# A blocked triangular inverse for two scan directions: one direction's right factor moved to the other partition half, its products to the off-diagonal array quarters

## The chip, the cores and the metric

The kernel runs on one core of a Trainium2 chip, in one launch. A core has TensorE (PE), VectorE (DVE), ScalarE (ACT), GpSimd (POOL) and SyncE (SP, which issues the DMAs here). The metric is device time in microseconds (us) of the whole kernel.

## What is computed

Two layers of an encoder over two sequences of 256 tokens, width 1024, in float32. Layer 0 mixes tokens by a linear recurrence in both directions, layer 1 by attention; a gated MLP follows each. Only the recurrence matters here. For each of 16 heads of 64 channels, and for each direction:

```python
def step(S, inp):
    r_t, w_t, k_t, v_t, a_t, b_t = inp
    sa = jnp.einsum('bhij,bhj->bhi', S, a_t)
    S = S * w_t[:, :, None, :] + sa[..., None] * b_t[:, :, None, :] + v_t[..., None] * k_t[:, :, None, :]
    return S, jnp.einsum('bhij,bhj->bhi', S, r_t)
...
y = (_wkv_scan(r4, dec4[0], kd4[0], v4, -kk, kk * a4[0], reverse=False)
     + _wkv_scan(r4, dec4[1], kd4[1], v4, -kk, kk * a4[1], reverse=True))
```

## The kernel before

Activations lie transposed, channels on the 128 partitions, the 512 tokens of both sequences along the free dimension. A pair of heads fills the partitions: the first head has partitions 0 to 63, the second 64 to 127 (`halves`). The recurrence is worked in chunks of 64 tokens (`NCH` = 8). Within a chunk it is a unit triangular system of 64 x 64, for every chunk, head and direction `n`, and its inverse is built in five levels (`LEVELS`) that double the size of the inverted blocks. Three 64 x 64 matrices per chunk and direction take part: `nt` is the system, `mt` the inverse so far transposed, `mc` the inverse so far, and `xc` holds the masked product between them. One level is: `xc` = mask(`nt`^T `mc`), the system product (`level_system`, L753 to L762); new `mc` = `mt`^T `xc`, the factor product (`level_factors`, L772); new `mt` = `xc`^T `mt`, the transposed factor (L778, not at the last level). Ahead of level 0 `first_factors` (L744) transposes `mt` into the first `mc`.

Each product is, for one direction, 16 calls of 64 x 64 x 64 in float32: 8 chunks times two heads. The profile has two matmul instructions for each call. A call reads both operands from one head's 64 partitions and writes the same 64 partitions of PSUM, so it uses one of the two diagonal 64 x 64 quarters of the array. Direction 0 goes to PSUM bank 4 (`mt`: bank 2), direction 1 to bank 5 (bank 3).

The other engines take the results out. DVE multiplies `xc` out of PSUM with a mask (L1778) and copies direction 1's `mt` (L1806). ACT copies both `mc` (L1309 for the first, L1322) and direction 0's `mt` (L1328); at the last level the result is `mf` (L1325). POOL makes the first `mt` from the system (`ident`, L1999 and L2002).

The pairs of heads run through a pipeline of stages, `stage(i)`, written out by hand for each engine: stage i scans pair i (`scans`), solves the triangular system of pair i+1 (`solves`), prepares pair i+2 (`prepares`) and normalises the output of pair i-1 (`norms_`). Every engine works in the order written. Between the products of a level PE does pieces of the scan (`solved`, `next_state`, `from_state`, `outputs`) and of the preparation (`key_scales` L675, `lora_rates` and `lora_decays` L659, `bonus_sum` L695); DVE and ACT do likewise (sigmoids L1254, exponentials from L1275, scans L1682 and L1687, the bonus L1698 and L1701, the prepared factors L1712 to L1717). At the end of a stage `grams` (L796, L800) and `transposed` (L814) make the operands of the next scan.

Six stages also carry two halves of an adaLN modulation: a matrix product L556 (`modulation_half`), an ACT copy of its row, a selection on PE (L710, `select_half`), and an ACT copy of the columns. Its weights come through one buffer, which SP fills again when a half's matmuls are done. All of these, the key scales, the LoRA products and the bonus sum share PSUM bank 7, and `key_scales` waits until the modulation columns of the stage before have been copied (`ada_taken`).

## Time and profile before

| | us |
|---|---|
| median of 3 runs | 2025.67 |
| lowest and highest | 2021.66, 2025.8 |
| the profiled execution | 2024.68 |
| its span, first to last instruction | 2022.9 |
| recurrence stages, first system product to the last stage | 252.7 to about 845 |
| one full stage (system product to system product) | 72.5 to 74.9 |

In the rows further down, L-numbers are lines of the kernel before; "PEld" is a weight load, "PE" a matmul. A matmul row of the timeline covers instructions of one line and form that follow each other: its start, its time to the end of the last one, their count (x32 is 16 calls). The number in brackets is how long the engine had been idle and what released it. Instructions of TensorE overlap, so that a row's time includes the tail of its last instruction, and the distance between the starts of two rows is what the first of them takes of the engine's time. The granted clock is a share of 2.4 GHz; it is 1.00 or 0.50.

### The profile page before, as it was taken

To read this page: it belongs to the slowest core of one execution; us is meant where nothing else is said; L and a number is where in the kernel's file an instruction comes from. 1 tells how busy PE (TensorE), PEld (TensorE's weight loads), DVE (VectorE), ACT (ScalarE), POOL (GpSimd) and SP (SyncE) were. 2 spreads that over 40 slices of the span, in tenths; PEclk is the share of its full clock that TensorE was granted. 3 is DMA by queue.
4 is the path that set the end of the run, shared out by engine and by line. 5 is a ranking of instruction groups with operands and counts; after the bars stand their busy time and mean duration, and the time that the engine had idled before them with its cause. 6 is when DMAs were issued, how large, how long until landed. Compare 5 with 4: busy or idle time off the path is not lost.

```text
span 2022.9 us, 45036 instructions
## 1 busy us (share of the span) xinstructions
PE 1782.7 (88%) x19956; PEld 1419.1 (70%) x19956; DVE 888.0 (44%) x1127; ACT 720.3 (36%) x1096; POOL 609.7 (30%) x314
## 2 busy tenths in 40 slices
PE   5999589899999899787999999978686789999995
PEld 2777278788888789564777788855565568888884
DVE  3755544454454454426333442035674454444203
ACT  3322233333333332235433332224343354444221
POOL 1332222222222220033333344443111434434433
PEclk8999789999999999898999999989798889999998
DMA  7330000110110100143556233211111213333221
GB/s 293 94 124 21 26 7 7 45 40 18 45 50 8 44 26 5 47 164 146 213 202 246 76 101 112 93 36 47 36 32 42 73 52 93 93 93 105 100 86 42
DMA packets 43881, 161.08 MB, mean 80 GB/s; under 512 B 3664, under 2 KB 18256, under 8 KB 40912
## 3 DMA queue, kind: packets, MB, share of 16 engines
q1 hardware_dynamic: 43728, 158.75, 23.0%
q8 instruction: 132, 2.16, 0.5%
q14 instruction: 21, 0.17, 0.0%
HBM read 156.64 MB, written 2.10 MB: 78 GB/s over the span
## 4 chain that ended last, share of the span: by engine, by line
PE 79%; DVE 11%; ACT 4%; POOL 3%; issue 2%; DMA 1%; ACTq 0%; DVEq 0%; SPq 0%; POOLq 0%
PE ps L529 14%; PE ps L530 14%; PE ps L531 14%; PE ps L772 4%; PE ps L778 3%; PE ps L760 2%; PE ps L630 2%; PE ps L631 2%; PE ps L632 2%; PE ps L556 2%; PE ps L814 2%; DVE x_res L1534 2%; PE ps L796 1%; DVE area L1464 1%; DVE area L1874 1%
## 5 line engine op out<-in xcount | busy, mean ns | idle before, releaser
L1952 POOL TENSOR_TENSOR split_w<-raw_w,split_w 128x1024 fp32r<-128x1024 f32 (+1 forms) x148 | 380.6, 2571 | 743.2 <-ACT split_w L1118 743.2
L530 PE MATMUL ps<-h_lo_pad,split_w 128*128 128x512 f32 x800 | 321.3, 402 | 0.0
L529 PE MATMUL ps<-h_hi,split_w 128*128 128x512 f32 x704 | 283.4, 403 | 17.7 <-DVE h_lo_pad L1473 17.7
L1118 ACT ACTIVATE split_w<-raw_w 128x1024 fp32r<-128x1024 f32 (+1 forms) x148 | 167.2, 1130 | 355.8 <-PE ps L531 355.6
L531 PE MATMUL ps<-h_hi,split_w 128*128 128x512 f32 x704 | 279.5, 397 | 0.0
L529 PE MATMUL ps<-ff_hi,split_w 128*128 128x512 f32 x448 | 178.8, 399 | 8.9 <-DVE h_lo_pad L1473 8.9
L529 PEld LDWEIGHTS ps<-h_hi,split_w 128*128 128x128 f32 x704 | 133.8, 190 | 68.8 <-issue 29.1
L531 PE MATMUL ps<-ff_hi,split_w 128*128 128x512 f32 x448 | 175.8, 393 | 0.0
L530 PEld LDWEIGHTS ps<-h_lo_pad,split_w 128*128 128x128 f32 x800 | 152.1, 190 | 33.7 <-issue 0.5
L1548 DVE SCALAR_TENSOR_TENSOR ffs<-ffs,fcur 128x512 f32<-128x512 f32 x44 | 82.5, 1876 | 176.5 <-ACT ffs L1151 176.5
L531 PEld LDWEIGHTS ps<-h_hi,split_w 128*128 128x128 f32 x704 | 133.0, 189 | 31.9
L1513 DVE TENSOR_TENSOR sx<-sx,ffs 128x512 f32<-128x512 f32 x32 | 22.2, 693 | 289.1 <-ACT ffs L1086 289.1
L530 PE MATMUL ps<-ff_lo,split_w 128*128 128x512 f32 x352 | 136.9, 389 | 0.0
L529 PEld LDWEIGHTS ps<-ff_hi,split_w 128*128 128x128 f32 x448 | 84.9, 190 | 30.7 <-issue 9.2
L772 PEld LDWEIGHTS ps<-area 64*64 64x64 f32 x2560 | 88.3, 144 | 17.1 <-issue 16.6
L772 PE MATMUL ps<-area 64*64 64x64 f32 x2560 | 95.8, 229 | 4.0 <-DVE area L1778 3.8
L531 PEld LDWEIGHTS ps<-ff_hi,split_w 128*128 128x128 f32 x448 | 84.8, 189 | 18.4
L1991 POOL TENSOR_TENSOR split_p<-o_res,split_p 128x1024 fp32r<-128x1024 f32 x24 | 57.9, 2413 | 129.3 <-ACT split_p L1229 129.3
L630 PE MATMUL ps<-x_split,split_p 128*128 128x512 f32 x192 | 78.4, 408 | 18.6 <-DVE x_split L1608 10.1
L1322 ACT ACTIVATE area<-ps 128x512 f32<-128x512 f32 x64 | 38.2, 597 | 147.8 <-PE ps L772 147.8
L760 PEld LDWEIGHTS ps<-area 64*64 64x64 f32 x2560 | 79.2, 136 | 10.6 <-issue 10.6
L1556 DVE TENSOR_TENSOR ffs<-ffs,ps 128x512 f32<-128x512 f32 x44 | 30.3, 688 | 123.6 <-ACT ffs L1155 123.6
(255 smaller groups left out, 3248.7 us busy)
## 6 DMA issues: line engine op xcount, KB each, us to landing
raw_w<-in_ffn_up SPq DMA_DIRECT2D x88, 512.0 KB, 3.7
raw_w<-in_ffn_down SPq DMA_DIRECT2D x32, 704.0 KB, 4.0
late_a<-in_ada_w SPq DMA_DIRECT2D x7, 2048.0 KB, 8.1
late_b<-in_ada_w SPq DMA_DIRECT2D x7, 2048.0 KB, 8.0
o_res<-in_proj_w SPq DMA_DIRECT2D x24, 512.0 KB, 3.7
area<-in_ada_w SPq DMA_DIRECT2D x12, 1024.0 KB, 6.1
area<-in_ada_w SPq DMA_DIRECT2D x4, 2048.0 KB, 21.2
x_res<-in_xT SPq DMA_DIRECT2D x2, 2048.0 KB, 11.4
```

The lines of the kernel that those rows point to most:

```text
L529: mm(bank, wh[:, o:o + P], hi[:, t], start=(t == 0), stop=False)
L530: mm(bank, wh[:, o:o + P], lo[:, t], start=False, stop=False)
L531: last = mm(bank, wl[:, o:o + P], hi[:, t], start=False, stop=(t == total - 1))
L556: last = mm(bank[g:g + CG, :], csil[:, k, :], blk[:, k, :], start=(k < NCG), stop=(k >= KT - NCG))
L630: mm(ps[:, m, :], wh[:, o:o + P], xh, start=(k == 0), stop=False)
L760: last = mm(ps[lo:hi, 4 + n, c * C:(c + 1) * C], nt[lo:hi, n, c, :], mc[lo:hi, n, c, :], start=True, stop=True)
L772: last = mm(ps[lo:hi, 4 + n, c * C:(c + 1) * C], mt[lo:hi, n, c, :], xc[lo:hi, n, c, :], start=True, stop=True)
L778: last = mm(ps[lo:hi, 2 + n, c * C:(c + 1) * C], xc[lo:hi, n, c, :], mt[lo:hi, n, c, :], start=True, stop=True)
L1118: A(split_w[:, r % 2, 0, 0:cols], raw_w[:, r, 0:cols], ACT.Copy).then_inc(w_hi, 1)
L1548: own(V.scalar_tensor_tensor(seqs(conv[s]), u_pad[s][:, :, 0:SEQ], fcur[:, s, 0:1], seqs(conv[s]), ALU.mult, ALU.add))
L1952: G.tensor_tensor(split_w[:, r % 2, 1, 0:cols], raw_w[:, r, 0:cols], split_w[:, r % 2, 0, 0:cols].bitcast(F32), ALU.subtract).then_inc(w_l ...
L1991: G.tensor_tensor(split_p[:, n % 2, 1], raw_p[:, n % NRAW, :], split_p[:, n % 2, 0].bitcast(F32), ALU.subtract).then_inc(proj_lo, 1)
```

## The change

For direction 1 the masked product `xc` and the factor `mt` lie on the other partition half: what belongs to the first head is on partitions 64 to 127, and the reverse. `nt` and `mc` stay. So direction 1's system product reads one half and writes the other, and its factor product goes back; both use the off-diagonal quarters. The calls of the two directions alternate, and the two last of them signal. The first `mt` of direction 1 is made by POOL in `xc`, brought to the other half by 16 products with the identity, and copied by DVE into `mt`. Bank 5 has what direction 1 writes across, bank 4 what direction 0 writes.

Other work is moved. On PE the first modulation half leaves level 4 and stands behind `outputs`, the second stands behind `transposed`, and the second selection stands in level 0 of the next stage, ahead of `key_scales`; ACT's copies move with them. The bonus of pair 0 on PE and DVE moves from ahead of the stages into the first stage.

```diff
+        across = ((0, C, C, P), (C, P, 0, C))
...
             def first_factors(q):
...
+                pe.wait_ge(ident_in, 2 * q + 2)
+                for c in range(NCH):
+                    o = slice(c * C, (c + 1) * C)
+                    for lo, hi, a, b in across:
+                        swapped = mm(ps[a:b, 5, o], ident[lo:hi, lo:hi], xc[lo:hi, 1, c, :], start=True, stop=True)
+                        last = mm(ps[lo:hi, 3, o], xc[lo:hi, 1, c, :], ident[lo:hi, lo:hi], start=True, stop=True)
+                    if c == NCH - 1:
+                        swapped.then_inc(side_mm, 1)
+                last.then_inc(mmm[1], 1)
 
             def level_system(q, l):
 
                 for n in range(NDIR):
                     pe.wait_ge(mev[n], LEVELS * q + l + 1)
-                    for c in range(NCH):
-                        for lo, hi in halves:
-                            last = mm(ps[lo:hi, 4 + n, c * C:(c + 1) * C], nt[lo:hi, n, c, :], mc[lo:hi, n, c, :],
-                                      start=True, stop=True)
-                    last.then_inc(xmm[n], 1)
+                if l == 0:
+                    pe.wait_ge(side_in, q + 1)
+                for c in range(NCH):
+                    o = slice(c * C, (c + 1) * C)
+                    for lo, hi, a, b in across:
+                        one = mm(ps[lo:hi, 4, o], nt[lo:hi, 0, c, :], mc[lo:hi, 0, c, :], start=True, stop=True)
+                        two = mm(ps[a:b, 5, o], nt[lo:hi, 1, c, :], mc[lo:hi, 1, c, :], start=True, stop=True)
+                one.then_inc(xmm[0], 1)
+                two.then_inc(xmm[1], 1)
...
             def level_factors(q, l):
...
                     pe.wait_ge(xev[n], LEVELS * q + l + 1)
-                    for c in range(NCH):
-                        for lo, hi in halves:
-                            last = mm(ps[lo:hi, 4 + n, c * C:(c + 1) * C], mt[lo:hi, n, c, :], xc[lo:hi, n, c, :],
-                                      start=True, stop=True)
-                    last.then_inc(mmm[n] if l < LEVELS - 1 else fmm[n], 1)
-                    if l < LEVELS - 1:
+                for c in range(NCH):
+                    o = slice(c * C, (c + 1) * C)
+                    for lo, hi, a, b in across:
+                        one = mm(ps[lo:hi, 4, o], mt[lo:hi, 0, c, :], xc[lo:hi, 0, c, :], start=True, stop=True)
+                        two = mm(ps[a:b, 5, o], mt[lo:hi, 1, c, :], xc[lo:hi, 1, c, :], start=True, stop=True)
...
+                if q == 0:
+                    bonus_sum(0)
...
+                        if 0 <= b < ADA_PAIRS:
+                            select_half(2 * b + 1)
                         if prepares:
                             key_scales(r)
...
-                        if ada_:
-                            modulation_half(2 * p)
...
-                    elif ada_:
-                        select_half(2 * p)
                 if scans:
                     outputs(p)
                 if ada_:
-                    modulation_half(2 * p + 1)
+                    modulation_half(2 * p)
                 if solves:
                     grams(q)
                 if ada_:
-                    select_half(2 * p + 1)
+                    select_half(2 * p)
                 if solves:
                     transposed(q)
+                if ada_:
+                    modulation_half(2 * p + 1)
...
+                if solves:
+                    dve.wait_ge(side_mm, q + 1)
+                    V.tensor_copy(mt[:, 1], chunks(ps[:, 5, :])).then_inc(side_in, 1)
                 for l in range(LEVELS):
...
-                    G.tensor_tensor(mt[:, n], nt[:, n], m1, ALU.mult).then_inc(ident_in, 1)
+                    G.tensor_tensor(xc[:, 1] if n else mt[:, 0], nt[:, n], m1, ALU.mult).then_inc(ident_in, 1)
```

In the following rows a count is of calls; the sizes are those of the output. PE at level 0 of the stage that starts at 611 us, before: L760 is the system product, L860 a piece of the scan, L724 the variance of the pair before, L675 the key scales, L772 and L778 the factor product and the transposed factor of direction 0, then of direction 1.

```order
L760 MATMUL ps<-area 64x64 x32
L860 MATMUL ps<-area 64x64 x8
L724 MATMUL ps<-area,ct 128x512
L675 MATMUL ps<-area 128x256 x2
L772 MATMUL ps<-area 64x64 x16
L778 MATMUL ps<-area 64x64 x16
L772 MATMUL ps<-area 64x64 x16
L778 MATMUL ps<-area 64x64 x16
```

The same place after the change; L772 and L773 (now the system product of direction 0 and of 1) and L786 and L787 (the factor product) alternate to 16 calls each, of which the last two and the first two stand here. L876, L726 and L677 are L860, L724 and L675.

```order
L772 MATMUL ps<-area 64x64
L773 MATMUL ps<-area 64x64
L876 MATMUL ps<-area 64x64 x8
L726 MATMUL ps<-area,ct 128x512
L712 MATMUL ps<-ct,area 128x2 x2
L677 MATMUL ps<-area 128x256 x2
L786 MATMUL ps<-area 64x64
L787 MATMUL ps<-area 64x64
```

The products of the two directions stand call by call in turn, and a selection (L712) stands between the variance and the key scales.

PE at level 4 and the end of the same stage, before: L841 is the scan, L556 and L710 the modulation, L772 the last factor product, L872 to L884 the outputs, L796 and L800 the grams, L814 the transposes.

```order
L841 MATMUL ps<-area 64x64 x8
L556 MATMUL ps<-area,csil 32x256 x8
L772 MATMUL ps<-area 64x64 x32
L710 MATMUL ps<-ct,area 128x2 x2
L872 MATMUL ps<-x_res,sx 64x64 x24
L878 MATMUL ps<-area 64x64 x32
L884 MATMUL ps<-area 64x64 x32
L556 MATMUL ps<-area,csil 32x256 x8
L796 MATMUL ps<-area 64x128 x32
L800 MATMUL ps<-area 64x64 x32
L710 MATMUL ps<-ct,area 128x2 x2
L814 MATMUL ps<-ct,area 64x64 x80
```

After the change, from the outputs (L888) on:

```order
L888 MATMUL ps<-x_res,sx 64x64 x24
L894 MATMUL ps<-area 64x64 x32
L900 MATMUL ps<-area 64x64 x32
L558 MATMUL ps<-area,csil 32x256 x8
L812 MATMUL ps<-area 64x128 x32
L816 MATMUL ps<-area 64x64 x32
L712 MATMUL ps<-ct,area 128x2 x2
L830 MATMUL ps<-ct,area 64x64 x80
L558 MATMUL ps<-area,csil 32x256 x8
L742 MATMUL ps<-x_res 64x64 x32
```

Ahead of the outputs there is now no modulation and no selection between the scan and the last factor product; one modulation half stands between the outputs and the grams, and the other between the transposes and the next system product.

## Rows read from the trace of the kernel before

**Rows 1.** The page, part 4: the chain that ended last, by engine.
```profile
PE 79%; DVE 11%; ACT 4%; POOL 3%; issue 2%; DMA 1%; ACTq 0%; DVEq 0%; SPq 0%; POOLq 0%
```
**Rows 2.** Busy us by stage: stretch, length, each engine (instructions), clock, DMA.
```profile
252.70:315.80 63.10, 53.27 (x1328) 48.88 (x1328) 27.94 (x44) 20.64 (x33) 15.74 (x12) 0.86 0.03 6
...
463.90:536.40 72.50, 66.96 (x1852) 59.22 (x1852) 36.39 (x57) 26.32 (x45) 16.30 (x12) 1.00 0.12 36
...
611.00:685.10 74.10, 68.52 (x1852) 60.72 (x1852) 36.40 (x57) 26.39 (x45) 16.30 (x12) 0.98 0.11 35
...
685.10:758.50 73.40, 67.22 (x1852) 59.38 (x1852) 36.39 (x57) 26.32 (x45) 16.30 (x12) 1.00 0.06 19
```
**Rows 3.** Timeline, level 0 of the stage at 611 us: start, us, engine, line, operation, count [idle].
```profile
618.21 1.15 PE L750 MATMUL ps<-ct,area 64*64 64x64 f32 x32 [1.13 <-POOL area L2002]
...
619.19 2.03 PE L760 MATMUL ps<-area 64*64 64x64 f32 x64
...
619.41 0.60 ACT L1309 ACTIVATE area<-ps 128x512 f32<-128x512 f32 x1 [1.68 <-PE ps L750]
...
621.06 0.63 PE L860 MATMUL ps<-area 64*64 64x64 f32 x16
```
**Rows 4.** Timeline, products on row halves and column groups.
```profile
613.48 1.12 PE L719 MATMUL ps<-o_res,ct 128*128 128x512 f32 x2
...
628.40 1.13 PE L659 MATMUL ps<-area 64*128 64x512 f32 x4
...
662.14 1.07 PE L556 MATMUL ps<-area,csil 128*32 128x256 f32 x16 [2.71 <-DVE area L1701]
```
**Rows 5.** Timeline, level 4 of that stage: evictions, factor product, select.
```profile
659.87 1.28 DVE L1778 TENSOR_TENSOR area<-ps,ct 128x512 f32<-128x512 f32 x2
...
663.14 3.46 PE L772 MATMUL ps<-area 64*64 64x64 f32 x64
...
666.53 0.75 PE L710 MATMUL ps<-ct,area 128*128 128x2 f32 x4
```
**Rows 6.** Timeline, level 1: PE behind the sigmoids.
```profile
632.24 0.68 PE L841 MATMUL ps<-area 64*64 64x64 f32 x16 [0.70 <-ACT h_pad L1254]
```
**Rows 7.** Timeline, level 2: evictions and factor product.
```profile
641.32 1.28 DVE L1778 TENSOR_TENSOR area<-ps,ct 128x512 f32<-128x512 f32 x2
...
642.15 1.15 PE L772 MATMUL ps<-area 64*64 64x64 f32 x32
```
**Rows 8.** Timeline, level 3: system product, second eviction, bonus sum.
```profile
647.77 2.08 PE L760 MATMUL ps<-area 64*64 64x64 f32 x64
...
649.89 0.69 DVE L1778 TENSOR_TENSOR area<-ps,ct 128x512 f32<-128x512 f32 x1 [0.24 <-PE ps L760]
...
651.63 1.12 PE L695 MATMUL ps<-h_pad,ct 128*128 128x512 f32 x2 [0.25 <-DVE h_pad L1698]
```
**Rows 9.** Timeline, start of the stage.
```profile
611.00 2.08 PE L740 MATMUL ps<-area 64*64 64x64 f32 x64 [0.70 <-ACT area L1355]
```
**Rows 10.** DMA issues: target, queue, count, KB each, median us to landing.
```profile
area<-in_ada_w SPq DMA_DIRECT2D x12, 1024.0 KB, 6.1
```
**Rows 11.** Timeline, stage at 758.5 us: first system product, last factor product.
```profile
766.69 2.03 PE L760 MATMUL ps<-area 64*64 64x64 f32 x64
...
800.41 2.03 PE L772 MATMUL ps<-area 64*64 64x64 f32 x64
```
**Rows 12.** Timeline, stage at 252.7 us: last factor product.
```profile
298.98 3.68 PE L772 MATMUL ps<-area 64*64 64x64 f32 x64 [3.15 <-DVE area L1778]
```
**Rows 13.** Timeline, ahead of the stage at 252.7 us and into it.
```profile
247.85 0.69 DVE L1701 SCALAR_TENSOR_TENSOR area<-ps,area 128x512 f32<-128x512 f32 x1 [2.17 <-PE ps L695]
...
248.84 1.79 POOL L2021 TENSOR_TENSOR x_res<-h_pad 128x512 f32<-128x512 f32 x1
...
252.71 3.68 PE L740 MATMUL ps<-x_res 64*64 64x64 f32 x64 [4.90 <-DVE x_res L1717]
...
258.16 1.97 PE L750 MATMUL ps<-ct,area 64*64 64x64 f32 x32 [1.77 <-POOL area L2002]
```

More of the change, by code:

```diff
@@ L333, in encoder_trunk @@
         tr, tr_in, ident_in = sem("tr"), sem("tr_in"), sem("ident_in")
+        side_mm, side_in = sem("side_mm"), sem("side_in")
         xmm, xev, mmm, mev = (pair_of(n) for n in ("xmm", "xev", "mmm", "mev"))
@@ L744, in first_factors @@
             def first_factors(q):
-                for n in range(NDIR):
-                    pe.wait_ge(ident_in, 2 * q + n + 1)
-                    for c in range(NCH):
-                        for lo, hi in halves:
-                            last = mm(ps[lo:hi, 2 + n, c * C:(c + 1) * C], mt[lo:hi, n, c, :], ident[lo:hi, lo:hi],
-                                      start=True, stop=True)
-                    last.then_inc(mmm[n], 1)
+                pe.wait_ge(ident_in, 2 * q + 1)
+                for c in range(NCH):
+                    for lo, hi in halves:
+                        last = mm(ps[lo:hi, 2, c * C:(c + 1) * C], mt[lo:hi, 0, c, :], ident[lo:hi, lo:hi], start=True, stop=True)
+                last.then_inc(mmm[0], 1)
+                pe.wait_ge(ident_in, 2 * q + 2)
[7 more added lines that the diff above has]
+                last.then_inc(mmm[1], 1)
             def level_system(q, l):
@@ L769, in level_factors @@
                     pe.wait_ge(xev[n], LEVELS * q + l + 1)
-                    for c in range(NCH):
-                        for lo, hi in halves:
-                            last = mm(ps[lo:hi, 4 + n, c * C:(c + 1) * C], mt[lo:hi, n, c, :], xc[lo:hi, n, c, :],
-                                      start=True, stop=True)
-                    last.then_inc(mmm[n] if l < LEVELS - 1 else fmm[n], 1)
-                    if l < LEVELS - 1:
+                for c in range(NCH):
+                    o = slice(c * C, (c + 1) * C)
+                    for lo, hi, a, b in across:
+                        one = mm(ps[lo:hi, 4, o], mt[lo:hi, 0, c, :], xc[lo:hi, 0, c, :], start=True, stop=True)
+                        two = mm(ps[a:b, 5, o], mt[lo:hi, 1, c, :], xc[lo:hi, 1, c, :], start=True, stop=True)
+                one.then_inc(mmm[0] if l < LEVELS - 1 else fmm[0], 1)
+                two.then_inc(mmm[1] if l < LEVELS - 1 else fmm[1], 1)
+                if l < LEVELS - 1:
+                    for n in range(NDIR):
                         for c in range(NCH):
@@ L972, in _ @@
             lora_rates(0, (7, 1))
-            bonus_sum(0)
             for i in range(-1, KT + 1):
@@ L1300, in stage @@
                 ada_ = scans and prepares
+                if 0 <= b < ADA_PAIRS:
+                    modulation_row(2 * b + 1)
                 if scans:
@@ L1310, in stage @@
                 for l in range(LEVELS):
+                    if l == 0 and 0 <= b < ADA_PAIRS:
+                        modulation_columns(2 * b + 1)
                     if l == 0 and norms_:
@@ L1315, in stage @@
                         right_sides(p, 2)
-                    if l == 4 and ada_:
-                        modulation_row(2 * p)
                     if solves:
@@ L1342, in stage @@
                     elif l == 4:
-                        if ada_:
-                            modulation_columns(2 * p)
                         if prepares:
@@ L1350, in stage @@
                 if ada_:
-                    modulation_row(2 * p + 1)
+                    modulation_row(2 * p)
                 if solves:
@@ L1356, in stage @@
                         if g == 0 and ada_:
-                            modulation_columns(2 * p + 1)
+                            modulation_columns(2 * p)
             decays(0, (2, 3), 0)
@@ L1765, in stage @@
                         V.tensor_tensor(nt[:, n, :, :], chunks(ps[:, 2 + n, :]), msk, ALU.mult).then_inc(sys_in, 1)
+                if q == 0:
+                    bonus(0, 1)
                 if prepares:
@@ L1840, in _ @@
             decays_back(0)
-            bonus(0, 0)
-            bonus(0, 1)
             products(0, 0)
             products(0, 1)
+            bonus(0, 0)
             for i in range(-1, KT + 1):
```

## The prediction

> **What bounds the kernel now.** I read the chain that ended last first: TensorE (PE) holds 79% of it, VectorE (DVE) 11% [rows 1]. The change touches only the recurrence between about 250 and 818 us, so next came the busy time by stage [rows 2]: three full stages of it take 72.5, 74.1 and 73.4 us, in which PE is busy for 67 to 69 us, DVE for 36, ScalarE (ACT) for 26. PE is the bound, yet not everywhere: the timeline of one stage (the one from 611.00 to 685.10 us) shows the places at which it waits, and the sum below is made there.
>
> **What one product costs, and what it can cost.** One direction of one level product is 16 calls, 32 instructions of a 64x64 quarter. Both directions take from 619.19 (L760) to 621.06 us (L860 behind it), 1.87 us for 64 instructions, 29 ns each [rows 3]. A 128x512 product of 2 instructions takes 1.12 us including its tail, L719 [rows 4], so an instruction streams 512 columns in at most 0.56 us, 64 columns in some 53 to 70 ns. At 29 ns apiece two quarters must be running at once: they share neither rows nor columns of the array. Do quarters that share rows run at once? L556 is 16 instructions of 256 columns in four column groups, all on the same 128 rows: 1.07 us, where one after the other they would take more than 3 [rows 4]. Quarters that share columns and not rows: L659, 4 instructions of 512 columns in two row halves, takes 1.13 us, as long as the two of L719 [rows 4]. The change needs both at once, with the two row halves writing different banks (4 and 5), as L659's also do. So I take four at a time: 64 instructions in 0.93 us. No row shows it for 64x64 quarters; the other end is 1.87 us (nothing gained). I take the end that L556 and L659 lie nearest to.
>
> There is a rule against this. In the rows a quarter starts an instruction every 58 ns, about its streaming time, so its weight loads cost nothing extra [rows 3, 4]. The Trainium skill (TensorE: Matmul & The Clock Gate, Part 3, "The mechanism") says that a weight load overlaps a running matmul only where the row group differs, by which quarters in the same rows would take turns and the pair stay at 1.87 us; the trace disagrees already with L556's 16 loads and products in one row group. What the sum would be by that rule is rival 1's.
>
> **The walk through the stage at 611 us.** "Lead" is how much earlier PE is than before.
> - Level 0. First factors: direction 0 as before; direction 1 is now 32 calls on four quarters, 0.93 us as its 16 on two were, started by the same GpSimd operation that releases L750 [rows 3]. The level's products now wait for both ACT evictions and the new DVE copy. Before, they began under the second eviction (619.19 against ACT 619.41 to 620.01 [rows 3]). The copy is a 128x512 one, 0.69 us like its neighbours on DVE, beside ACT's 0.60. It is queued ahead of DVE's first eviction of the level, which waits for PE anyway. Lead -0.9.
> - System product +0.93. The select moved in here from the end and its ACT copy must land before the key scales: some 0.75 us by L710 [rows 5], taken whole. Factor product +0.93. Lead +0.2.
> - Level 1. The system product hides nothing: PE waits 0.70 us for ACT's sigmoids before L841 [rows 6] and will wait longer. Factor product +0.93. Lead 1.1.
> - Level 2. DVE is late here: its rates run until the evictions at 641.32, and PE's factors start at 642.15 after the first of the two [rows 7]. Now they need both (to 642.60): -0.5, and the system product is again hidden. Factor +0.93. Lead 1.5.
> - Level 3. From the system product's start to the end of the second eviction was 2.8 us (647.77 to 650.58 [rows 8]) and becomes 0.93 + 0.25 + 0.69 + 0.24 + 0.69 = 2.8: the halved product is eaten by evicting both directions after it. L1698 and the bonus sum L695 behind them keep lead 1.5. Factor +0.93. Lead 2.4.
> - Level 4. DVE's backward scan runs ahead of the evictions and starts from PE's last transposed-factor product, so the evictions end 2.4 earlier than 661.15, at 658.75 [rows 5]. Before, PE then also waited for L1701 and ran the modulation half (662.14), and started the factors at 663.14 [rows 4, 5]. With the modulation gone from here they start at 658.8: lead 4.35. They took 3.39 us (663.14 to 666.53) at half clock [rows 5]; PE's wait ahead of them stays near 2.9 us, so I leave them half clocked: 1.7 for 3.39, +1.7, and the select after them (0.67) leaves too. Lead 6.6 or so.
> - End. The modulation half and select around the grams stay, with the other half's numbers. The second half now stands behind the transposes: +1.0 us, from L556 to L772 [rows 4, 5], of which 0.70 covers PE's wait for the last ACT copy [rows 9]. Its weights are fetched after the first half's matmuls, some 11 us earlier, and fetches of that kind land in 6.1 us [rows 10]. Lead 6.3.
>
> Two of the six stages of this kind ran at full clock throughout (463.90 and 685.10 us, clock 1.00 [rows 2]). There the factor product of level 4 saves 0.93 and the select 0.54, so 5.6. Sum: 4 x 6.3 + 2 x 5.6 = 36.4 us.
>
> **The other stages.** Stage 758.5 (no preparation, hence none of the ACT and DVE waits above): five factor products +4.65; level 0 -0.9 and -0.5 for the last select; from system start to factor start, five times, the new 2.85 stands against 3.5, 3.7, 2.3, 3.5 and 2.3 us (first at 766.69, the last ending at 800.41 [rows 11]), +1.0. About +4.3. Stage 252.7 has no scan work between its products, so ACT and DVE set the pace: factor products give some 0.6 net in four levels, and the last, 3.4 us at half clock [rows 12], 1.6, against -0.9 at level 0: +3.3, between 2 and 5. Ahead of it the bonus of pair 0 leaves DVE's path to the first system product: DVE waited 2.17 us for PE's sum and then ran L1701, 0.69, with its first half ahead of that; but GpSimd's last product ended at 250.63 and the first system product started at 252.71 [rows 13], so only about 2.0 come back. The sum now runs under GpSimd's identity steps, which PE waits for anyway, 1.77 us [rows 13]; if they don't cover it, 1 us is lost again.
>
> Total: 36.4 + 4.3 + 3.3 + 2.0 = 46 us. The profiled execution took 2024.68 (span 2022.9 and 1.8 around it); its sum is 1978.7. The median of the runs shown is 1.0 above, so 1979.
>
> **Rivals.**
> 1. *Quarters in the same rows take turns*, so the change doesn't do what it says: the pair stays at 1.87 us. For it: no row shows four 64x64 quarters. Against: L556. Then the walk loses 0.93 at eight places (first factors, system product of levels 0 and 3, five factor products), 7.4 a stage: 6.1 - 7.4 = -1.3, six times -8; stage 758.5 gets 4.3 - 8.4, stage 252.7 3.3 - 6.5, the start keeps 2. Sum -13: 2039, **slower**. It decides from about 1.7 us for a pair on, where the eight places eat the whole 6.1.
> 2. *PE can't start instructions that fast.* The quickest sustained row starts one per 29 ns; four quarters want one per 14.6, with a weight load each. For it: no row is faster over 32 instructions. Against: L556's groups start together. Half-way, at 1.4 us for a pair, half of the 59 us between the two sums, 46 gained and 13 lost, is gone: 2009. The Trainium skill (the same page, "Wait - 56ns, not 53.3ns?") has starts never closer than about 25 ns however small the matmul; by that a pair would take 1.6 us (an estimate from that page) and the sum come to about 2021; no run here shows the floor, since the array's own time is above it.
> 3. *The clock.* PE's waits grow at levels 0 to 3 while its work shrinks; after the wait of 2.7 us at level 4 the factor product took 3.39 us instead of 1.87 (1.2 instead of 2.4 GHz) [rows 4, 5]. If two more such stretches come in each of eight stages, at 1.7 us each, 27 us go: 2006. For it: the 2.9 us wait recurs in every stage. Against: waits of 1.1 us at level 0 [rows 3] left the clock at full speed.
>
> **Chances.** Forecast 0.70, rival 1 0.08, rival 2 0.10, rival 3 0.12. A measurement of this kernel can tell 0.2% (4 us) from no change. Faster: forecast, rival 3 and half of rival 2, with a little of the rest to spare: 0.87; same 0.04; slower 0.09. Range: below, all level-4 products at full clock and no select wait, 6 stages x 2 us, 1966; above, rivals 2 (half-way) and 3 with a few us: 2012.
>
> **What would show it.** Level products of both directions in 0.93 us for 64 instructions (right) or 1.87 (rival 1) or between (rival 2). PE's waits: about 1 us before level 0's system product, 1.7 before L841 and before level 2's factors, 2.9 before level 4's. Stages of 66 to 69 us. Half-clock stretches other than at level 4 would speak for rival 3. The forecast is wrong if the pairs halve and a stage still takes over 71 us; then evictions, not products, set the levels.

## The result

The changed kernel takes 1999.38 us (median of 4 runs, 1991.52 to 2002.33) beside 2023.66 us for the kernel before in the same session: ratio 0.9875, 95% interval 0.9842 to 0.9907. It is faster, inside the range, by 24 us where 46 were forecast. Measured again beside the experiments it gave 1996.29 us, ratio 0.9867 (0.9847 to 0.9888). The profiled execution took 1991.52 us, span 1989.7. What lies behind the solving stages is untouched by the change, but takes 1206 us in this profile and 1212 us in another of the same kernel (1210 us before), so below I compare stages, not spans. The seven stages from the first system product on take 505.8 us before and 476.1 us after: 29.7 us gained, where the prediction had 36.4 + 3.3.

Busy time by stage after, columns as in [rows 2]: the stage at 252.6, three full ones, and the last solving one (728.7 us).

```profile
252.60:312.50 59.90, 43.62 (x1360) 37.51 (x1360) 30.09 (x47) 20.10 (x33) 15.48 (x12) 0.90 0.03 7
449.80:520.00 70.20, 61.09 (x1888) 53.15 (x1884) 36.69 (x58) 25.95 (x45) 16.30 (x12) 0.95 0.12 37
589.80:660.30 70.50, 61.51 (x1889) 53.65 (x1885) 36.79 (x58) 25.85 (x45) 16.08 (x12) 0.95 0.12 37
660.30:728.70 68.40, 59.14 (x1888) 51.71 (x1884) 36.81 (x58) 25.84 (x45) 16.31 (x12) 0.98 0.12 35
728.70:778.10 49.40, 41.29 (x1550) 37.75 (x1548) 20.02 (x30) 13.27 (x25) 5.03 (x4) 1.00 0.02 5
```

PE is busy for 59 to 62 us of these three full stages, 67 to 69 before [rows 2]: the halved products are there. But the stage shrinks by 4.4 us on average, not by 7, and in two of these three the clock is at 0.95. In the last solving stage PE's busy time falls from 47.77 to 41.29 us and its length rises, 48.9 to 49.4 us.

Now the halved product itself: PE by line in 3 us around level 0's system product, stage at 660.3 us (line, names, shape, count, busy us, mean ns of one, idle before). L772 is direction 0, L773 direction 1.

```profile
L772 PE MATMUL ps<-area 64*64 64x64 f32 x32 | 1.2, 222 | 0.9 <-DVE area L1793 0.9
L773 PE MATMUL ps<-area 64*64 64x64 f32 x32 | 1.2, 223 | 0.0
```

Each has its 32 instructions within 1.2 us including the tail of the last one, and both lie in the same 1.2 us. From the start of the pair to the start of the product behind it (L876) it is 0.95 us, some 15 ns for each of the 64. Before, 64 took 2.03 with the tail [rows 3], 1.87 from start to start. Four 64x64 quarters do run at once. The rest of this text asks why that did not become time.

PE's waits between 315 and 775 us after (who, what for: us in total, times, longest):

```profile
PE ps L786 <- DVE area L1800: 27.5, 14, 2.8
PE ps L857 <- ACT h_pad L1271: 9.7, 6, 1.6
PE ps L757 <- POOL area L2023: 8.2, 7, 1.4
PE ps L772 <- DVE area L1793: 6.2, 7, 0.9
PE ps L697 <- DVE h_pad L1715: 5.5, 6, 1.9
```

L786 is the factor product of levels 2 and 4, waiting for DVE's evictions of both system products: 27.5 us. In the same stretch of the kernel before the largest was the modulation's wait for L1701, 16.2 us in all, six of the kind in [rows 4].

### The profile page after: what moved, and what is told of

The parts are those of the page before. It is cut to its first block, busy times and chain, and to the rows that moved or that the text cites. A ratio compares the mean times of both kernels' runs of the same rounds, so it can differ in the third digit from the quotient of the medians.

```text
span 1989.7 us, 45604 instructions
## 1 busy us (share of the span) xinstructions
PE 1711.0 (86%) x20212; PEld 1347.5 (68%) x20212; DVE 892.4 (45%) x1135; ACT 716.4 (36%) x1096; POOL 609.7 (31%) x314
## 4 chain that ended last, share of the span: by engine, by line
PE 76%; DVE 13%; ACT 4%; POOL 3%; issue 2%; DMA 1%; ACTq 0%; DVEq 0%; SPq 0%; POOLq 0%
PE ps L531 14%; PE ps L532 14%; PE ps L533 14%; PE ps L794 3%; PE ps L632 2%; PE ps L633 2%; PE ps L634 2%; PE ps L558 2%; PE ps L830 2%; DVE x_res L1551 2%; DVE area L1800 1%; DVE area L1895 1%; PE ps L786 1%; PE ps L812 1%; DVE area L1481 1%
## 5 line engine op out<-in xcount | busy, mean ns | idle before, releaser
L531 PEld LDWEIGHTS ps<-h_hi,split_w 128*128 128x128 f32 x704 | 133.7, 190 | 69.6 <-issue 29.5
L632 PE MATMUL ps<-x_split,split_p 128*128 128x512 f32 x192 | 78.5, 409 | 18.6 <-DVE x_split L1625 10.1
L786 PE MATMUL ps<-area 64*64 64x64 f32 x1280 | 50.7, 231 | 36.7 <-DVE area L1800 36.6
L1103 ACT ACTIVATE ffs<-ps 128x512 f32<-128x512 f32 x32 | 19.1, 598 | 164.9 <-PE ps L533 164.9
L633 PE MATMUL ps<-x_split,split_p 128*128 128x512 f32 x192 | 77.8, 405 | 0.0
L786 PEld LDWEIGHTS ps<-area 64*64 64x64 f32 x1280 | 45.5, 144 | 47.7 <-issue 47.5
```

Of the source, the lines that this page charges most:

```text
L531: mm(bank, wh[:, o:o + P], hi[:, t], start=(t == 0), stop=False)
L632: mm(ps[:, m, :], wh[:, o:o + P], xh, start=(k == 0), stop=False)
L633: mm(ps[:, m, :], wh[:, o:o + P], xl, start=False, stop=False)
L786: one = mm(ps[lo:hi, 4, o], mt[lo:hi, 0, c, :], xc[lo:hi, 0, c, :], start=True, stop=True)
```

## The experiments

Stages are counted as the prediction did: six full ones (from 312.5 us on), one ahead of them, one last. "Stages" in the table is the sum of the first seven in the profiled execution; "half clock" is how many stretches with a granted clock of 0.50 lie in the six full ones; "L4" is PE's wait ahead of level 4's factor product in a middle stage.

| kernel | us, median | ratio (95%) | stages, us | half clock | L4, us |
|---|---|---|---|---|---|
| before | 2023.66 | 1 | 505.8 | 4 | (2.7, modulation) |
| changed | 1999.38 | 0.9875 (0.9842 to 0.9907) | 476.1 | 8 | 2.8 |
| changed again (a1) | 1996.29 | 0.9867 (0.9847 to 0.9888) | 476.5 | 7 | 2.8 |
| e1 products alone | 2014.89 | 0.9971 (0.9959 to 0.9983) | 496.3 | 8, longer | 3.6 (modulation) |
| e2 moves alone | 2004.04 | 0.9914 (0.9901 to 0.9928) | 486.6 | 0 | 1.3 |
| e4 shift by DVE | 1992.52 | 0.987 (0.9846 to 0.9894) | 472.9 | 6 | 2.8 |
| e5 scan later | 1977.85 | 0.979 (0.9772 to 0.9807) | 461.3 | 2 | 1.0 |
| e6 moves, scan later | 1991.83 | 0.9854 (0.9837 to 0.987) | 476.4 | 0 | none |
| e7 system in turns | 1983.08 | 0.9809 (0.9793 to 0.9826) | 468.6 | 3 | 2.2 |
| e8 = e7 with scan later | 1970.45 | 0.9754 (0.9737 to 0.977) | 453.4 | 0 | 0.6 |
| e9 = e8 with shift by DVE | 1967.71 | 0.9742 (0.9726 to 0.9759) | 451.6 | 0 | 0.6 |
| e10 factor in turns | 2005.36 | 0.9909 (0.9876 to 0.9942) | 488.9 | 7 | 2.2 |

In the expectations, M says that the moves bring most of the gain, S (called F in the later ones) that PE's instructions come too slowly, C that the clock takes the gain, W that it is lost in waits of PE for ACT and DVE. A "stop" is a wait of PE that the profile puts down to no engine ("issue").

**The change split in two, and the whole again.** e1 has the products on four quarters and the side copy, with the modulation halves, their selects and the first bonus at their old places. e2 has these at their new places and the products of before. The heart of e2:

```diff
-                for c in range(NCH):
-                    o = slice(c * C, (c + 1) * C)
-                    for lo, hi, a, b in across:
-                        one = mm(ps[lo:hi, 4, o], mt[lo:hi, 0, c, :], xc[lo:hi, 0, c, :], start=True, stop=True)
-                        two = mm(ps[a:b, 5, o], mt[lo:hi, 1, c, :], xc[lo:hi, 1, c, :], start=True, stop=True)
+                    for c in range(NCH):
+                        for lo, hi in halves:
+                            last = mm(ps[lo:hi, 4 + n, c * C:(c + 1) * C], mt[lo:hi, n, c, :], xc[lo:hi, n, c, :],
+                                      start=True, stop=True)
```

> The changed kernel once more, for a second trace and its spread. Theory S (supply): the two quarters now started beside the other two use up TensorE's instructions faster than they are fetched, so the trace shows stops inside products that no semaphore explains, 8 to 12 us between 310 and 780 us, at other places than in the first trace except in the last solving stage, and times spread over 1991 to 2003 us. Theory C (clock): no such stops beyond 2 us; the spread comes from the number of half-clock stretches between 310 and 780 us (nine of 3.4 us in the first trace, four before).

> Only the products of the levels on four quarters, the modulation and the bonus at their old places. By the walk it loses the 2.0 us at level 4 and gains back the 0.75 us of the select in six stages, and about 0.7 at the start: 8 us slower than the changed kernel, 0.992 of before. If the moved work is what brings the gain (theory M), 0.996 or above.

> Only the moves (modulation, selects, bonus of pair 0), the products on two quarters as before. By the walk 2.0 - 0.75 - 0.3 in six stages and 0.7 at the start: 6 to 7 us, 0.997 of before. Theory M: 0.992 or below.

The changed kernel repeats. Between 310 and 780 us its second trace has 9.7 us of stops, within the 8 to 12 of theory S; the first has 6.3 us. Theory C had no more than 2 us of stops; the half-clock stretches that it speaks of are there as well. The split surprised me: the moves alone give 0.86%, the products alone 0.29%. The prediction's walk, which has the moves at some 2 us of a stage's 6, would have it the other way round; both results lie where theory M had them. With the moves a full stage takes 70.4 us at full clock, as here at 597.0 us:

```profile
597.00:667.40 70.40, 66.61 (x1856) 59.27 (x1852) 36.96 (x57) 26.40 (x45) 16.30 (x12) 1.00 0.12 37
```

and putting four-quarter products on top brings only another 1 us a stage. PE is busy for 66.61 of 70.40 us there: little is left to wait for. With the four-quarter products (the rows at the top) it is busy for 59 to 62 of about 69.

**What a long run of such instructions gives.** e3 adds, behind the last stage, three streams on PE that wait for nothing and whose results nothing reads (a single run, 2099.99 us): 640 calls on four quarters with 64 columns, 640 on four quarters with 128 columns, and 640 on two quarters with 64.

```diff
+            def four_wide():
+                for c in range(160):
+                    o = slice(c % NCH * C, (c % NCH + 1) * C)
+                    for lo, hi, a, b in across:
+                        mm(ps[lo:hi, 4, o], weights(lo, hi), ct[lo:hi, K_COS:K_COS + C], start=True, stop=True)
+                        mm(ps[a:b, 5, o], weights(lo, hi), ct[lo:hi, K_COS:K_COS + C], start=True, stop=True)
```

> The changed kernel with three streams of products behind the recurrence, whose results nobody reads: 640 calls of 64 columns on four quarters, 640 calls of 128 columns on four quarters, 640 calls of 64 columns on two. No waits inside. By the array alone 18.7, 35.7 and 37.3 us. Theory S: instructions come in 16 KB packets (256 instructions, 64 calls) no closer than 3.4 to 3.9 us in the traces, so the first stream takes 30 to 38 us after a quick start, and the other two, which need a packet per 3.6 and 3.7 us, are little or not slowed. Theory C: 19 us for the first.

The three streams by length, columns as in [rows 2], and PE's waits in the first:

```profile
821.30:859.30 38.00, 24.42 (x1277) 23.21 (x1279) 8.18 (x10) 1.58 (x2) 2.35 (x1) 0.87 0.17 59
859.30:898.00 38.70, 37.08 (x1298) 35.20 (x1293) 0.00 (x0) 0.00 (x0) 0.00 (x0) 1.00 0.02 4
898.00:935.40 37.40, 37.40 (x1290) 37.36 (x1280) 0.00 (x0) 0.00 (x0) 0.00 (x0) 1.00 0.02 5
...
PE ps L910 <- issue: 13.6, 8, 2.6
```

38.0, 38.7 and 37.4 us for the same 1280 matmuls and 1280 weight loads: four quarters, four quarters with twice the columns, two quarters. Twice the columns, or half the quarters, fit into the same time: 66 to 68 instructions a microsecond pass. (The first stretch also has loads for the next phase in it, and pieces at half clock.) In the first stream PE is busy for 24.42 us and stands 13.6 us in 8 stops that wait for no engine ("issue"). Between two stops lie 128 matmuls (once 256), 1.87 us long at 14.6 ns each; with their weight loads that is 256 instructions. The DMA table of the same three stretches has the queue that brings instructions (queue, packets, MB, share):

```profile
q8 instruction: 9, 0.15, 1.7%
...
q8 instruction: 10, 0.16, 1.8%
...
q8 instruction: 11, 0.18, 1.9%
```

Packets of 16 KB, one for each 256 instructions, 3.4 to 4.2 us apart. Two quarters use a packet up in 3.73 us and never notice. The second stream, with a DMA share of 0.02, still has stops:

```profile
PE ps L917 <- issue: 1.5, 4, 0.6
```

Four quarters with 64 columns use a packet up in 1.87 us and then stop, once what was fetched ahead is gone. So a pair of products does run in 0.95 us, as a burst; a stage full of pairs has a floor of its own. That the packets set the pace is inferred from their spacing and the equal times of the streams; no run changed the rate of fetching.

**Where the waits hit.** Four kernels undo one thing each. e5 moves one call of DVE's program (three operations, the backward scan and what follows it) behind the evictions of level 4:

```diff
                         if prepares:
                             bonus(r, 1)
+                            decays_back(r)
...
-                    elif l == 3:
-                        if prepares:
-                            decays_back(r)
```

> The changed kernel with one step of DVE moved: the backward scan and the two operations after it (2.6 us) stand behind DVE's evictions of level 4 and not ahead of them, in the seven stages that prepare the next pair. TensorE's wait ahead of level 4's factor product, 2.8 to 3.0 us, should shrink to about 1.1. Theory W: TensorE gains 1.8 us a stage there, 13 us, and as the long wait goes, the half-clock stretch of 3.4 us that follows it in the changed kernel goes too, 0.9 us and more each, 6 to 10 us: 13 to 23 us less, ratio 0.976 to 0.981. Theory F: the time won runs into stops for instructions (more of them in the streams of outputs, grams and transposes behind level 4), about half of it stays: 7 to 12 us, ratio 0.981 to 0.984.

e6 is the same edit on e2.

> The moves alone, with products on two quarters as before (ratio 0.9914 when last measured), and the same step of DVE moved as in e5_scan_later. There the wait at level 4 was 1.5 us and the clock stayed at full speed, so only some 1.2 us a stage are to be had, 8 us: ratio 0.987. The distance to e5_scan_later says what the four-quarter products are worth once the long wait is out of the way: by theory W it grows from 0.4 to 0.8% and more (13 us of array time a stage less can then be used), by theory F it stays at 0.4% or falls, since the supply of instructions and not the array is the limit.

DVE in the changed kernel ahead of level 4 (stage at 660.3 us), and what PE says of its wait there:

```profile
704.09 1.21 DVE L1704 TENSOR_TENSOR_SCAN area<-ct,area 128x512 f32<-128x512 f32 x1
705.34 0.69 DVE L1707 TENSOR_TENSOR area<-area 128x512 f32<-128x512 f32 x1
706.06 0.69 DVE L1709 TENSOR_TENSOR area<-area 128x512 f32<-128x512 f32 x1
706.67 1.28 DVE L1800 TENSOR_TENSOR area<-ps,ct 128x512 f32<-128x512 f32 x2
...
PE ps L786 <- DVE area L1800: 2.8, 1, 2.8
```

Three operations, 2.6 us, ahead of the two evictions that PE waits for. In e5 the wait at this place is 1.0 us, and the kernel is 0.8% faster than the changed one: theory W's range, 0.976 to 0.981. e6 gains too, though less, and the distance between four quarters and two (e5 against e6) is 0.64%, where it was 0.4 to 0.5% (the changed kernel against e2). W had more than 0.8 there, F at most 0.4. The intervals, 0.2% and more on each side, don't decide that; in the traces the distance of the seven stages grows from 10 to 15 us.

The other part of e5's gain is the clock. Three stretches of 3.2 to 3.4 us around that wait in the changed kernel, then three around the same place in e2 (where the wait is 1.3 us), columns as in [rows 2]; the clock is the third number from the end:

```profile
704.90:708.10 3.20, 0.41 (x14) 0.30 (x11) 3.13 (x6) 2.51 (x4) 1.75 (x2) 1.00 0.02 5
708.50:711.90 3.40, 3.40 (x98) 3.40 (x90) 0.38 (x1) 2.10 (x4) 1.03 (x2) 0.50 0.03 7
711.90:715.30 3.40, 3.40 (x121) 3.40 (x120) 3.06 (x8) 0.65 (x2) 2.60 (x2) 0.99 0.02 5
...
714.50:717.80 3.30, 2.07 (x72) 1.93 (x67) 3.23 (x6) 3.23 (x5) 1.11 (x1) 1.00 0.00 0
717.80:721.20 3.40, 3.36 (x115) 3.39 (x117) 1.42 (x3) 1.84 (x4) 1.70 (x3) 1.00 0.03 7
721.20:724.60 3.40, 3.40 (x124) 3.40 (x121) 3.24 (x3) 1.02 (x2) 2.97 (x2) 1.00 0.02 5
```

In this stage, where PE was busy for 0.41 us of 3.2, the clock fell from 2.4 to 1.2 GHz right behind, under the factor product and the scan's outputs: these two then took 1.36 and 6.24 us instead of 0.94 and 5.12 (the same two in e7's last full stage, at full clock), 1.5 us lost. In e2 it stayed. Such a wait is not always followed by a fall: of the six full stages of the changed kernel, with 2.6 to 2.8 us at this place, five have a half-clock stretch behind it; the stage at 520.0 us, with 2.8 us, has none.

e7 leaves the factor products on four quarters and makes the system products of one direction after the other, as before:

```diff
                 for n in range(NDIR):
                     pe.wait_ge(mev[n], LEVELS * q + l + 1)
+                    if l == 0 and n:
+                        pe.wait_ge(side_in, q + 1)
+                    for c in range(NCH):
+                        o = slice(c * C, (c + 1) * C)
+                        for lo, hi, a, b in across:
+                            out = ps[a:b, 5, o] if n else ps[lo:hi, 4, o]
+                            last = mm(out, nt[lo:hi, n, c, :], mc[lo:hi, n, c, :], start=True, stop=True)
+                    last.then_inc(xmm[n], 1)
```

> The changed kernel, but each level's system product is made one direction after the other on two quarters (1.87 us for both instead of 0.93), direction 0 waiting for its own eviction only; the factor products stay on four quarters. The walk of the prediction gives the halved system products 0.93 us a stage at levels 0 and 2 each and nothing elsewhere, so 1 to 2 us a stage would be lost: ratio 0.993 to 0.997. Theory W: nothing is lost where DVE's two evictions follow anyway, and level 0 starts earlier under the second ACT eviction: 0 to 5 us faster, ratio 0.9845 to 0.987. Theory F adds that the stops inside the products' streams become fewer, since 128 instructions now take 1.87 us: also at or below the changed kernel.

> The counterpart of e7: the changed kernel with its system products on four quarters at once, and its factor products of one direction after the other on two quarters. With the moves alone (0.9914), e7 (four quarters for the factors alone, 0.981) and the changed kernel (both, 0.987) this fills the square. If system products on four quarters are worth nothing and cost the wait for both evictions at level 0 (theory W), it is slower than the moves alone by as much as the changed kernel is slower than e7, 0.4 to 0.7%: ratio 0.994 to 0.998. By the walk of the prediction the halved system products give 1 to 2 us a stage: 0.985 to 0.988.

e7 is 0.6% faster than the changed kernel: half as many quarters in five products of ten, and less time, more than either theory had. In its last full stage (652.9 us) the factor product of level 4 starts 47.74 us into the stage, in the changed kernel's 47.80: up to there the halved system products had gained nothing. DVE evicts the two directions one after the other, and with the products in turn the first eviction runs under the second product. What differs comes behind: the wait is 2.2 us there instead of 2.8, and in this stage the clock stays up.

```profile
652.90:719.70 66.80, 60.77 (x1890) 53.37 (x1886) 37.82 (x58) 25.84 (x45) 16.59 (x12) 1.00 0.12 36
```

Against 68.40 us and 0.98 in the changed kernel's row at the top. Over the six full stages e7 is 8.4 us shorter. It has three half-clock stretches there, all at this wait of 2.2 us; the changed kernel has five at it, two at level 0 and one at level 3. e10, the other way round (system products on four quarters, factor products in turn), gives 0.9909, no different from the moves alone. It lies between the two ranges of the expectation, and its interval reaches both. So of the four-quarter products those of the factors alone are worth 1% and those of the systems alone nothing that shows, and with both the systems take 0.6% back.

**Fewer instructions.** e4 makes direction 1's shifted factor with two DVE copies inside SBUF instead of 16 PE products and a copy out of PSUM:

```diff
-                        swapped = mm(ps[a:b, 5, o], ident[lo:hi, lo:hi], xc[lo:hi, 1, c, :], start=True, stop=True)
...
-                    dve.wait_ge(side_mm, q + 1)
-                    V.tensor_copy(mt[:, 1], chunks(ps[:, 5, :])).then_inc(side_in, 1)
+                    dve.wait_ge(ident_in, 2 * q + 2)
+                    for lo, hi, a, b_ in across:
+                        V.tensor_copy(mt[a:b_, 1], xc[lo:hi, 1]).then_inc(side_in, 1)
```

> The changed kernel, with one part done otherwise: direction 1's first right factor is put on the other partition half by two DVE copies of 64x512 from SBUF instead of 16 TensorE products (64 of some 3790 TensorE instructions of a stage) and one copy out of PSUM; the first system product no longer waits for it, the first factor product does. Theory W (the products' gain is lost in waits of TensorE for ACT and DVE): in the changed kernel TensorE stands 1.1 us between the end of the first factors and level 0's system product; 0.4 to 1.1 us of each of eight stages comes back, 3 to 8 us: ratio to the kernel before 0.983 to 0.9855, where the changed kernel had 0.987. Theory F (TensorE's instructions come too slowly): a quarter of a block of 256 instructions less per stage, at some 3.7 us a block 0.9 us, but only where a stage stops for instructions: above all the last solving stage becomes 0.9 us shorter, all stages together 1 to 3 us: 0.9855 to 0.9865.

No difference that the times show: 0.987, with an interval that covers both theories' ranges. The last five full stages are 68.2 us each instead of 69.6, the two stages ahead of them 1.3 and 2.6 us longer. The first of these two has 10.2 us at half clock where the changed kernel has 6.8, the second has a half-clock stretch at level 0 where the changed kernel has one at level 3; why is open. PE's wait at level 0's system product, 6.2 us in all for the DVE copy in the changed kernel, is 5.5 us for ACT's second eviction now:

```profile
PE ps L766 <- ACT area L1324: 5.5, 7, 0.8
```

So the copy was not the price of that wait: without it PE waits there for ACT's eviction of the second direction.

**Both gains together.** e8 is e7 with e5's move, e9 adds e4's shift.

> The changed kernel with both edits that gained: system products of the two directions in turn on two quarters (0.981 alone), and DVE's backward scan behind its evictions of level 4 (0.979 alone; the changed kernel 0.987). They act at different places (levels 0 to 3; level 4). If each gain stands by itself, as theory W has it, the ratio is 0.973 (0.971 to 0.975). If the supply of instructions is what now sets most stages, theory F, the second gain is at most half: 0.975 to 0.978, with over 10 us of stops inside TensorE's streams.

> As e8_turns_and_scan_later, and direction 1's first right factor put on the other half by DVE from SBUF as in e4_shift_by_dve: 64 of some 3790 TensorE instructions of a stage fewer, and no wait of TensorE for that copy at level 0's second system product. In e4 this gave about 1 us in each of the later stages and lost 1.3 and 2.6 us in the first two. By theory W nothing changes by over 3 us against e8, since direction 0's product covers the wait; by theory F a quarter of a block less gives 0.5 to 0.9 us a stage, 4 to 7 us less than e8, ratio about 0.003 below it.

```profile
640.10:705.70 65.60, 61.11 (x1890) 53.56 (x1886) 38.25 (x58) 25.96 (x45) 16.86 (x12) 1.00 0.12 37
...
PE ps L785 <- DVE area L1799: 10.2, 14, 1.0
```

The row is a full stage of e8, then its wait for DVE's evictions between 315 and 775 us: 10.2 us in all where the changed kernel had 27.5. No half-clock stretch is left in the full stages. e8 takes 1970.45 us, 2.5% less than before and 1.2% less than the changed kernel; e9 takes 1967.71, whose interval overlaps e8's; W had no more than 3 us there, F 4 to 7. The two gains of e8 add up to 1.16% of the 1.4% that they give singly. The ratio lies in F's range, but its interval reaches into W's, and F's sign, over 10 us of stops, is not there: it has 5.1 us between 310 and 780. So this run does not decide between them. Both kernels beat the kernel before and the changed one.

e8 differs from e5 in the system products alone, which e8 makes in turn. The largest stops in the six full stages, first of e5, then of e8:

```profile
PE ps L794 <- issue: 1.8, 3, 0.9
PE ps L894 <- issue: 1.7, 3, 1.0
PE ps L888 <- issue: 1.6, 1, 1.6
PE ps L857 <- issue: 1.3, 2, 0.9
...
PE ps L893 <- issue: 0.7, 2, 0.5
PE ps L793 <- issue: 0.3, 1, 0.3
```

In all they are 7.6 us in e5 and 1.5 in e8, and e8's six full stages are 7.9 us shorter. So with four quarters for the system products too, stops cost time in the full stages as well; that they are the supply of instructions is inferred from e3.

## Why the prediction was right, and where it was not

**The halved pair: right.** 0.95 us for 64 instructions, forecast 0.93. Rival 1, that quarters in the same rows take turns, is out, and with it the rule on row groups that it was worked out for. The floor of 25 ns between starts, which rival 2 cites, does not hold across quarters either: some 15 ns on average.

**The walk through a stage: right where nothing disturbs it.** The stage at 685.10 us before [rows 2] and at 660.3 us after are the same stage; before, it has no half-clock stretch, after, one behind level 4. The four waits that the prediction named came as well (0.9, 1.6, 1.6 and 2.8 us for 1, 1.7, 1.7 and 2.9). PE's lead, as forecast for a stage at full clock and as the two timelines give it:

| place | forecast | measured |
|---|---|---|
| level 0, system product | -0.9 | -1.07 |
| level 0, factor product | -0.7 | -0.98 |
| level 1, system product | 0.2 | -0.05 |
| level 2, factor product | 0.6 | 0.28 |
| level 3, system product | 1.5 | 1.33 |
| level 3, factor product | 1.5 | 1.55 |
| level 4, system product | 2.4 | 2.60 |
| level 4, factor product | 4.35 | 4.33 |
| outputs | 5.8 | 5.50 |
| next stage | 5.6 | 4.98 |

**What failed in the six full stages: the clock, as a term of 4 x 6.3, and stops for instructions, which have no term.** The walk left level 4's factor product half clocked and let the stage behind it run as before. But the stretch moved: the products now end before it does, and it runs on over the outputs. And more of them came, 8 instead of 4 in the six full stages. Two are at level 0 (459.4 and 599.3 us), behind the waits for GpSimd and for both evictions, and cost those stages 1.5 and 1.7 us ahead of the first factor product; they gained 2.4 and 3.6 us in all. I had written that a wait of 1.1 us at level 0 left the clock alone. Now there are two (1.1 and 0.9 us) with a product of 0.93 us between them in each of the six stages, and the clock fell behind them in two. Rival 3 had the mechanism and named the place, but as two more stretches in each stage; two thirds of one came (4 in six).

The clock is not all of it. This stage has no half-clock stretch:

```profile
520.00:589.80 69.80, 59.39 (x1888) 51.12 (x1884) 37.61 (x58) 25.84 (x45) 16.58 (x12) 1.00 0.13 37
```

It gained 4.8 us instead of 6.3, and 1.7 us of stops lie in it. In a1 the stage at 449.3 us has 3.6 us of stops and takes 71.9 us, over the 71 that the prediction named as a sign of being wrong; there it is the stops, not the evictions. The six stages take 68.1 to 70.5 us, where 66 to 69 were forecast, and gained 26.5 us instead of 36.4; 2.2 us of stops lie in them here and 4.9 us in a1, with eight and seven half-clock stretches.

**What failed: the last solving stage, +4.3 us forecast, -0.5 measured.** This was counted as array time, since ACT and DVE have little to do there. PE's waits of that stage after:

```profile
PE ps L786 <- DVE area L1800: 2.0, 2, 1.0
PE ps L794 <- issue: 1.7, 1, 1.7
PE ps L888 <- issue: 1.1, 1, 1.1
PE ps L757 <- POOL area L2023: 1.1, 1, 1.1
PE ps L772 <- DVE area L1793: 0.9, 1, 0.9
PE ps L772 <- issue: 0.6, 1, 0.6
```

Before, and in e2, it has no "issue" at all. PE is idle for 8.1 us of it, 1.1 before: 2.9 us more for the evictions, which the forecast allowed for, and 4.1 us of stops (two small ones are not in the list), for which it has no term. Without them the stage would have gained some 3.6 us, an estimate from these rows. 12 packets of instructions arrive in its 49.4 us, 4.1 us each; at the 3.4 to 4.2 us of the streams 12 packets are 41 to 50 us. So the stage is near the rate at which its instructions come; that this rate is what stops it is inferred, as in the streams. In the kernels with four-quarter factor products it takes 54 to 56 us up to the transposes behind its grams, before 54.3 and in e2 54.6. Only e9, with fewer instructions, is below, 52.9; e4, with as few, is not (55.4), so the link to their number is likely and not shown. Rival 2 said that PE can't start instructions this fast. It was expected in the pair (0.93 or 1.4 us) and sits in the stage: bursts are fast, the mean is not.

**The split between the moves and the products: wrong, though the sum came near.** The walk books 1.95 us for the modulation leaving level 4. In e2 a stage like the one walked (597.0 us) is 3.7 us shorter than before, because with the modulation the long wait at level 4 goes, and with that the half-clock stretch. The four-quarter products bring both back: PE is early at level 4, stands there for 2.6 to 2.8 us, and in five of six full stages the clock falls behind it.

**The system products: right that they bring nothing.** The walk set 0.93 against a longer wait of 0.9 at level 0 and called the rest hidden or eaten (the expectation of e7 read it too kindly); e7 and e10 bear that out. Not seen was that they make PE early at level 4 and lengthen its wait from 2.2 to 2.8 us, that the clock pays for it in most stages, and that more stops come with them (e5 against e8).

**The start: 0.1 us gained instead of 2.0.** The bonus left DVE's path as forecast, but DVE's last operations, which the first system product waits for [rows 13], now wait for ACT and run beside GpSimd's product (the last row is that of the same copies before):

```profile
249.91 1.45 DVE L1732 COPY pend<-area 128x2 f32<-128x2 f32 x4 [3.05 <-ACT area L1295]
...
250.00 1.27 POOL L2042 TENSOR_TENSOR x_res<-h_pad 128x512 f32<-128x512 f32 x1
...
252.61 3.68 PE L742 MATMUL ps<-x_res 64*64 64x64 f32 x64 [17.92 <-DVE x_res L1734]
...
251.10 0.37 DVE L1715 COPY pend<-area 128x2 f32<-128x2 f32 x4
```

Four copies in 1.45 us where they took 0.37 without GpSimd beside them; the first system product starts at 252.61, before at 252.71 [rows 13]. In the other kernels of the table that have this move it starts between 251.05 and 252.75, so part of this is not the copies, and what it is stays open. The stage behind it gained 3.2 us (forecast 3.3). Up to the last solving stage's end the trace has 29.3 us of the forecast 46.

## What to carry to other kernels

A product that gets faster gives time only where its result is not the next thing waited for: before halving it, look at which engine takes the result out and what stands ahead of that in its queue; here moving one DVE call gave 0.8%, four quarters for the factor products 1%, for the system products nothing. Waits of TensorE can have a second price, the clock behind them, so an edit that only lengthens a wait can cost time. And count instructions as well as columns: many small matmuls on all quarters run into the rate at which instructions arrive.

## What the runs showed of the hardware

- Four 64x64 quarters, each with its own weights, run fp32 products at once: some 15 ns from start to start on average, a weight load with each, 0.95 us for 64 (128 in 1.87 us in e3).
- Such a stream lasts for the instructions fetched ahead and then goes at 66 to 68 instructions a microsecond: 1280 matmuls with their loads took 38.0 us on four quarters and 37.4 on two. Instructions came in packets of 16 KB, 3.4 to 4.2 us apart. The Trainium skill (Runtime: NRT & Kernel Launch, "Instruction fetch mechanics") has the refill in blocks of 16 KiB, 256 instructions, which agrees with the packets, and calls the cost of a block's end mostly hidden. The first stream disagrees, with 13.6 us of stops in 38.0.
- Waits of 2.6 to 2.8 us ahead of level 4's factor product were followed by 3.4 us at half clock in five of the six full stages of the changed kernel, waits of 2.2 us in three of six (e7); after waits of 1.0 to 1.3 us at the same place (e5, e2) the clock stayed at full speed in all six.
